# Three dense tiles' expert gates added to a DRAM table by GpSimd instead of built from one-hot products

## What is computed

```python
q = (h @ w_q).reshape(T, 8, 2, 128)
s = einsum('thpd,hpnd->thpn', q, sub_keys)            # scores of 2 x 128 sub-keys, 8 heads
vals, idx = top_k(s, 16)
cand = vals[:, :, 0, :, None] + vals[:, :, 1, None, :]
top_s, top_pos = top_k(cand.reshape(T, 8, 256), 16)
experts = i1 * 128 + i2                                # 16 of 16,384 experts per head
gates = softmax(top_s)                                 # (T, 8 * 16)
a = gelu(einsum('td,ted->te', h, u_tab[experts]))
y = einsum('te,ted->td', gates * a, v_tab[experts])
x = x + gate2 * rmsnorm(y)
```

## Time and profile before

| | us |
|---|---|
| runs | 2873.4, 2895.03, 2897.18 |
| median | 2895.03 |
| span of the profiled execution | 2847.3 |
| TensorE busy in it | 2774.5 |
| VectorE busy | 2158.4 |
| GpSimd busy | 1313.3 |
| ScalarE busy | 1249.3 |

### The profile page before, as it was taken

How to read it: one execution, slowest core, us unless ns; L and a number is a source line. 1 busy time by engine, 2 the same in 40 slices (tenths; PEclk the granted TensorE clock), 3 DMA queues, 4 the chain that set the end, 5 groups by cost and what they waited for, 6 DMA issues and landing times.

```text
span 2847.3 us, 43522 instructions
## 1 busy us (share of the span) xinstructions
PE 2774.5 (97%) x15948; PEld 2538.1 (89%) x15948; DVE 2158.4 (76%) x3708; ACT 1249.3 (44%) x2302; POOL 1313.3 (46%) x1036
## 2 busy tenths in 40 slices
PE   6998999999999999999999999999999999999998
PEld 5776778889999999999999999999998887877786
DVE  7655545887668778678989898777768878887888
ACT  4333662233357767744454544445522233332233
POOL 0002000000000000177878887777778888888884
PEclk9998999999999999999999999999999999999999
DMA  7520223225556566589898999899999999999996
GB/s 281 227 71 31 89 75 111 69 78 177 182 177 211 200 203 205 185 286 316 301 329 301 314 303 331 308 331 311 321 361 380 359 333 345 374 341 356 341 358 262
DMA packets 328417, 721.37 MB, mean 253 GB/s; under 512 B 44000, under 2 KB 159840, under 8 KB 326368
## 3 DMA queue, kind: packets, MB, share of 16 engines
q1 hardware_dynamic: 238176, 451.18, 44.9%
q0 software_dynamic: 90112, 268.76, 27.3%
HBM read 605.50 MB, written 114.30 MB: 253 GB/s over the span
## 4 chain that ended last, share of the span: by engine, by line
PE 57%; POOL 18%; issue 5%; DVE 2%; ACT 1%; DMA 1%; DVEq 0%; SPq 0%; ACTq 0%; POOLq 0%
PE mix L1434 47%; POOL picked_act L1872 9%; POOL rows L1879 9%; PE mix L116 5%; PE sps_all L1929 2%; PE sps_all L1947 1%; PE mix L1947 1%; ACT onehot L1641 1%; PE sps_all L1521 1%; DMA rows<-in_v,eidx 0%; DVE lo L106 0%; DVE onehot L1723 0%; DMA wq_raw<-in_w_q 0%; DVEq L1123 0%; ACT hi L101 0%
## 5 line engine op out<-in xcount | busy, mean ns | idle before, releaser
L1872 POOL DMA_INDIRECT picked_act<-act_early,aidx x384 | 467.0, 1216 | 1043.0 <-PE mix L1434 938.5
L1434 PE MATMUL mix<-a_hi,hi 128*128 128x320 f32 (+1 forms) x3072 | 810.1, 318 | 2.0 <-DVE lo L106 1.9
L1434 PE MATMUL mix<-a_lo,hi 128*128 128x320 f32 (+1 forms) x3072 | 808.8, 317 | 0.0
L1434 PE MATMUL mix<-a_hi,lo 128*128 128x320 f32 (+1 forms) x3072 | 808.5, 317 | 0.0
L1879 POOL DMA_INDIRECT rows<-in_v,eidx x512 | 651.3, 1272 | 166.4 <-issue 133.2
L1782 DVE SCALAR_TENSOR_TENSOR ys<-rows,coef,ys 128x1024 f32<-128x1024 f32 x504 | 633.9, 1284 | 118.6 <-DMA rows<-in_v,eidx 105.3
L106 DVE TENSOR_TENSOR lo<-raw,hi 128x1024 fp32r<-128x1024 f32 x384 | 469.2, 1222 | 301.4 <-ACT hi L101 301.0
L101 ACT ACTIVATE hi<-raw 128x1024 fp32r<-128x1024 f32 x384 | 404.8, 1054 | 358.3 <-PE mix L1947 348.3
L1434 PEld LDWEIGHTS mix<-a_hi,hi 128*128 128x128 f32 x3072 | 533.6, 188 | 3.2 <-ACT gelu L1650 2.3
L1434 PEld LDWEIGHTS mix<-a_lo,hi 128*128 128x128 f32 x3072 | 535.1, 188 | 0.0
L1434 PEld LDWEIGHTS mix<-a_hi,lo 128*128 128x128 f32 x3072 | 534.7, 188 | 0.0
(11 more groups left out here) (268 smaller groups left out, 3899.3 us busy)
## 6 DMA issues: line engine op xcount, KB each, us to landing
raw<-in_u SPq DMA_DIRECT2D x256, 512.0 KB, 4.9
raw<-in_v SPq DMA_DIRECT2D x128, 512.0 KB, 6.0
act_late<-gelu SPq DMA_DIRECT2D x128, 320.0 KB, 4.6
act_in<-act_late SPq DMA_DIRECT2D x128, 256.0 KB, 6.5
act_early<-gelu SPq DMA_DIRECT2D x128, 192.0 KB, 1.8
gate_d<-free_lo SPq DMA_DIRECT2D x19, 1024.0 KB, 8.1
gt<-gate_d SPq DMA_DIRECT2D x64, 256.0 KB
free_lo<-gate_d SPq DMA_DIRECT2D x64, 256.0 KB, 7.6
```

Of the source, the lines that this page charges most:

```text
L1434: done = pe.matmul(dst, w, a[:, k, cols], start=first, stop=last)
L1872: pool.indirect_dma_start(out=g.picked_act[:, e:e + 1], out_offset=None, in_=act_tables[e // (EARLY * CHOSEN)], in_offset=bass.IndirectOff ...
```

## The change

The gates of dense tiles are built in two ways instead of one. The dense tiles are now tiles 0 to 3 and the gathered ones 4 to 7. The tiles handled in retrieval (0 to 2) are thereby dense. For these GpSimd adds each gate, by an indirect transfer of one float for each of 128 tokens with an adding write, to a zeroed table in DRAM: 3 tiles x 8 heads x 16 choices = 384 transfers. The table lies beside the activations (`act_gates`, 512 activation columns and 384 gate columns per key and expert), so one load of 448 KB a step (`ag_in`) brings both. Tile 3 keeps the one-hot products: 16 batches, steps 49 to 94. Its gates are loaded as before, 64 KB a step. L1809's one multiplication becomes two (384 and 128 columns).

Four transfers on ScalarE's queue zero the table during the projections, and a GpSimd memset makes their source. The gates of the first tiles are finished by pairs of heads (`shift_heads`, `exp_heads`, `finish_heads`), three pairs in retrieval and the last in steps 6 to 8. Before head h of a tile is added, the previous head's sixteen transfers must have landed. Rows start at step 147 instead of 133; 2.5 fall in a step up to 255 (272 in all) and 1.9 behind it. Buffers move; the semaphores of the attention stage are freed and cleared behind it.

```diff
-HEAD_TILES = EARLY
+HEAD_TILES = DENSE - 1
+HEAD_GROUP = 2
+HEAD_EXPS_AT = (7, 11, 15)
...
+SCATTERED = HEAD_TILES
+AG = DTOK + SCATTERED * P
+ZERO_TILES, ZERO_COLS = 64, 192
+ZERO_FILLS = N // ZERO_TILES * SCATTERED * P // ZERO_COLS
+ZERO_AT = (3, 4, 5, 6)
+DENSE_FROM = 2 * N - 8
...
-ROWS_FROM, PICKS, BEATS = 133, 4, 4
-ROW_EVERY = (5 / 12, 7 / 12)
+ROWS_FROM, PICKS, BEATS = 147, 4, 4
+ROW_EVERY = (2 / 5, 10 / 19)
...
+            def clear_gates(j):
+                rows, part = divmod(j, SCATTERED * P // ZERO_COLS)
+                cols = slice(DTOK + part * ZERO_COLS, DTOK + (part + 1) * ZERO_COLS)
+                tables = g.act_gates[rows * ZERO_TILES:(rows + 1) * ZERO_TILES, :, cols].rearrange("n p c -> p n c")
+                if j == 0:
+                    act.wait_ge(g.zeros_ready, 1)
+                act.dma_start(tables, g.zeros[:].unsqueeze(1).to_broadcast([P, ZERO_TILES, ZERO_COLS])).then_inc(g.zeros_stored, 16)
...
+def finish_heads(g, dve, b):
+
+    gates = g.gates_d[:, 0:HEAD_TILES, group_heads(b), :]
+    norm = g.norm[:, 0:HEAD_TILES * HEAD_GROUP].rearrange("p (c h) -> p c h", h=HEAD_GROUP)
+    dve.wait_ge(g.heads_exps, b + 1)
+    dve.tensor_reduce(norm, gates, AX, ALU.add)
+    for h in range(HEAD_GROUP * b, HEAD_GROUP * (b + 1)):
+        dve.scalar_tensor_tensor(g.sidx[:, 0:HEAD_TILES, h, :], g.chosen_r[:, h, :, :, 1], float(NKEYS), g.chosen_r[:, h, :, :, 0],
+                                 ALU.mult, ALU.add)
+    dve.drain()
+    dve.reciprocal(norm, norm)
+    for c in range(HEAD_TILES):
+        slots = g.sidx[:, c, group_heads(b), :]
+        dve.tensor_scalar(slots, slots, float(AG), g.gate_col[:, c:c + 1], ALU.mult, ALU.add)
+    dve.drain()
+    dve.tensor_tensor(gates, gates, norm.unsqueeze(3).to_broadcast([P, HEAD_TILES, HEAD_GROUP, TOPK]), ALU.mult)\
+       .then_inc(g.scatter_ready, 1)
...
-    rows = 12 * (min(m, late) - ROWS_FROM + 1) // 5
-    return min(GATHERED * CHOSEN, rows + max(0, m - late) * 12 // 7)
+    rows = 5 * (min(m, late) - ROWS_FROM + 1) // 2
+    return min(GATHERED * CHOSEN, rows + max(0, m - late) * 19 // 10)
...
-        pieces = lambda a: a[:].rearrange("p (k j t) -> p k j t", k=KC, t=GTOK)
-        gates = g.gt[n // GROUP % 2].rearrange("p k (j n t) -> p k j n t", n=GROUP, t=GTOK)[:, :, :, n % GROUP, :]
-        dve.tensor_tensor(pieces(g.cf[n % 2]), gates, pieces(g.act_in[n % ACTS]), ALU.mult)\
-           .then_inc(g.cf_ready, 1)
+        both, cols = g.ag_in[n % ACTS], slice(SCATTERED * P, DTOK)
+        dve.tensor_tensor(g.cf[n % 2][:, 0:SCATTERED * P], both[:, 0:SCATTERED * P], both[:, DTOK:], ALU.mult)
+        pieces = lambda a: a.rearrange("p (j t) -> p j t", t=GTOK)
+        gates = g.gt[n // GROUP % 2].rearrange("p j (n t) -> p j n t", t=GTOK)[:, :, n % GROUP, :]
+        dve.tensor_tensor(pieces(g.cf[n % 2][:, cols]), gates, pieces(both[:, cols]), ALU.mult).then_inc(g.cf_ready, 1)
...
+    def scatter_gates(t, head):
+        if head:
+            pool.wait_ge(g.scattered[t], 16 * TOPK * head)
+        for k in range(TOPK):
+            pool.indirect_dma_start(out=gate_table, out_offset=bass.IndirectOffsetOnAxis(ap=g.sidx[:, t, head, k:k + 1], axis=0),
+                                    in_=g.gates_d[:, t, head, k:k + 1], in_offset=None, compute_op=ALU.add)\
+                .then_inc(g.scattered[t], 16)
+
+    for head in range(HEADS):
+        if head == 0:
+            pool.wait_ge(g.zeros_stored, 16 * ZERO_FILLS)
+        if head % HEAD_GROUP == 0:
+            pool.wait_ge(g.scatter_ready, head // HEAD_GROUP + 1)
+        for t in range(HEAD_TILES):
+            scatter_gates(t, head)
```

372 lines of the change are left out of this document (194 added, 178 removed).

## The result

Four runs of the changed kernel took 2997.3 to 3009.6 us, median **2999.6**; the kernel before took 2889.8 in the median of four. The ratio is **1.0396, 95% interval 1.036 to 1.0432**: slower by 4%. (The ratios are estimated from the single runs; the quotient of the medians can differ by a tenth or two of a per cent, and is 1.038 here.) The forecast was 2928 us and a range up to 2990.

A forecast was written before the change was run, and what follows sets the result against it. TensorE was taken to bound the kernel, with GpSimd setting the pace after the change. Terms -47 + 3 + 0 + 0 + 20 + 67 = +43, taken as +33: span 2880, plus 47.7 gives 2928 us, range 2846 to 2990.

The forecast's parts named there:

- What bounds the kernel: Whole kernel: TensorE, busy 97% of the span, so work taken off it shortens the span if its feeding engine keeps up.
- Removed from TensorE, -47: First and second sweep: 48 of 64 gate batches and three transposes go, 9.5 us in the first and 36.5 in the second.
- Retrieval, +3: Retrieval: VectorE's gate finishing per two heads takes about 3 us a group; only the third group is not hidden.
- Zero fills, 0: Projections: four 6.3 MB fills, 17 us of DMA each, cost nothing as weights load a tile ahead; upper end 68 us.
- The sign named for this: Projections: TensorE waiting on weights between 120 and 190 us would show the zero fills costing time.
- The scatters, 0: From 518 us: 384 adds at 1.49 us end near 1090, harmless up to 1.99 us each; 38 us per 0.1 beyond.
- Second sweep, +20: Second sweep: rows need a gather per 1.41 us, GpSimd takes 1.49; lateness between 0 and 35 us.
- Dense sweep, +67: Dense sweep: 468 gathers at 1.63 us plus 14 make 777 us against 710; range 0 to +123.
- Minus 10 for shared lateness: Second and dense sweeps: 10 us of the second's lateness is the same the dense would meet, so +43 becomes +33.
- 47.7 us outside the span: Whole kernel: the runs' median 2895.0 lies 47.7 us above the profiled span; the same was added to the forecast span.
- Scatters outlast the first rows: Rival, second sweep: at 2.2 us a scatter, rows start 80 us late, giving 3010 us; chance 0.10, including a costly fill.
- The rival of no change or faster: Dense sweep: GpSimd keeps up at a gather of 1.48 us, giving 2851 us, faster by 1.5%; chance 0.24.

The follow-up runs named there:

- a_no_scatters: The changed kernel without its 384 adding transfers and the waits for them (gates of three tiles missing): 2918.1 against 2853.5 us of the kernel before, 1.0229.
- two_scattered: A kernel computing the whole output: tiles 0 and 1 scattered, 2 and 3 by one-hot products, fills in pieces, against the kernel before: 2848.3 against 2855.7 us, 0.9979.
- a_third: The changed kernel, unedited, on a chip of the faster kind: 2943.7 against 2855.7 us of the kernel before, 1.0294.
- b_again: The kernel before, unedited, profiled and timed once more on a chip of the faster kind: 2855.5 us.
- a_fills_pieces: The changed kernel with its zero fills in 32 transfers of 0.79 MB from GpSimd, each after the last landed: 2929.4 against 2856.7 us of the kernel before, 1.0264.
- a_rows_151: The changed kernel with rows from step 151 instead of 147 and 2 instead of 1.9 in a dense step: 2948.2 against 2856.7 us of the kernel before, 1.0318.
- b_third: The kernel before, unedited, profiled on a chip of the slower kind: 2897.5 us.
- a_again: The changed kernel, unedited, on a chip of the slower kind: 3013.2 against 2897.7 us of the kernel before, 1.0386.
- b_rows_147: The kernel before with only the changed kernel's row schedule (rows from step 147 instead of 133): 2945.4 against 2853.5 us, 1.0328.
- a_one_input: The changed kernel with two VectorE instructions of a dense step reading one SBUF input instead of two (low products wrong): 2990.9 us against 3013.2 unedited.

## Why the prediction was wrong, step by step

On an A chip the parts can be set beside the forecast's: taken off TensorE 42 us (forecast 47), retrieval and fills +35 (3), second sweep +27 (20), dense sweep +74 (67), and nothing for shared lateness (-10). Together +94 in the span, forecast +33. Of these 61 us the fills are 32, more than half; the forecast's mechanism, that GpSimd sets the pace from the second sweep on, was right and its two large terms were each 7 us short.

*What bounds the kernel.* Right: in a_no_scatters and two_scattered what is taken off TensorE in the second sweep arrives in full, 901.1 instead of 938.3 us.

*Removed from TensorE, -47.* Right in the second sweep: -37.2 for 38 batches and three transposes. In the first sweep 5.2 arrive instead of 9.5. The rest is lost in the sweep's first 43 us, where TensorE is busy 37.1 us instead of 41.0 (a_third, b_again); why was not tried.

*Retrieval, +3.* It can't be read apart from the fills. With both it is +34.6, and +5.9 in a_fills_pieces, so +3 is not contradicted.

*Zero fills, 0.* **Failed, +34.6 or nearly.** I argued that a weight load a tile ahead absorbs being late by 17 us. The size was about right (25.17 MB at the stretch's 348 GB/s are 72 us in all, I had 68), the cover wasn't: the fills come one behind the other at 84, 97, 117 and 137 us, and TensorE waited 31.5 us for `w_lo`. The sign named for this, TensorE waiting on weights between 120 and 190 us, came. What runs showed instead: four fills delay the sweeps by 25 to 41 us at each of four places, and 28.7 us go with the same bytes in 32 pieces, one at a time. So it is not the bytes as such, and hardly the place.

*The scatters, 0.* **Failed by a term of its size.** I took 1.49 us each and named 1.99 as the limit of what does no harm. They took 1.742 + 0.304 = 2.05. The floor is 1.55 instead of the pick's 0.94. Started at 560 instead of 518 (35 of these 42 us are the later start of everything), they end at 1346, and the first row comes at 1364 instead of 1303. Of these 61 us 37 are the later start of the second sweep, the fills above all; against the steps the row is 24 us late (its due point, step 145.5, is at 1340). By my own rule of 38 us for each 0.1 us beyond the limit I would have had 23 us more; measured: 23 to 27 (a_no_scatters against a_third). The rule was about right, the price wrong. What the scatters cost on a B chip no pair of runs shows.

The line of the Trainium skill that I quoted against these adds (DMA: Bandwidth & Descriptors, Specifications: below 512 B a DMA engine reads, modifies and writes) speaks of the DMA engines, prices nothing and says nothing of GpSimd's time. By GpSimd's time the add does cost more than the plain write, 1.55 against 0.95 us. For the rest of the core it is the plain writes, at 1.3 us apart, that are the costly ones. Whether such a read and write takes place no run shows.

*Second sweep, +20.* The reason was wrong and the size near, which is luck. I had 1.19 us for a gather there; it took 1.13 in a_third and 1.10 to 1.11 in a_no_scatters and a_rows_151 (from 1400 us on), with issue 1.41, which is what the schedule wants. With rows on time none of the steps is late (a_no_scatters, a_rows_151: 0 us). The 27 us on an A chip go with the late first row.

*Dense sweep, +67.* **Right**: 74.3 on an A chip; on B chips 63.3 (the result's own profile against b_third) and 83.6 (a_again against it). The count was 465 instead of 468, a gather 1.645 to 1.70 instead of 1.63, and what follows the last gather 24 us instead of 14. b_rows_147 shows the whole of it by the schedule alone (+76.7). The reason given for 1.65, gathers held by VectorE's instructions with two SBUF inputs, was too narrow: a_one_input shows that one with one input holds them too.

*Minus 10 for shared lateness.* Not seen. The sweeps' losses add up.

*47.7 us outside the span.* **Failed.** Each run has 1.8 us there. I joined a span of one chip to a median of another. The forecast's increment doesn't hang on it, but the 40 us of a B chip are no constant either: the issue idle in them grows from 20 us to between 51 and 58.

*Chances.* "Scatters outlast the first rows" had 0.10 and only at 2.2 us; fills shared it. Both came, and together with the forecast's own mechanism. The range ended at 2990, below the 3010 us that this rival gave by itself, and had no room for two of these on top of each other. The rival of no change or faster needed a dense gather of 1.48; it was 1.65.

## What to carry to other kernels

Before work is moved to an engine, count that engine's budget to the end: here each gather put off costs 1.65 us and each scatter 2.05. A tile's 128 scatters take 262 us of GpSimd to save 16 of TensorE (16 batches of 0.96 us), and that pays only in time in which nobody else wants GpSimd. Price a bulk transfer by the small transfers that come behind it, not by its share of the bandwidth: cut in pieces, each issued when the one before had landed, the same bytes cost 6 us and not 35. And take the time outside the span from the run that was profiled, never from another.

## What the hardware showed that I had not expected

- Small writing transfers of GpSimd, one in about 1.3 us, nearly stop the core while the DMA engines are at 0.10: TensorE does one product in 0.6 us (655 to 862 us) to 2.8 us (950 to 1118), with nothing to wait for in the profile. The granted clock is at its lower level, 1.2 GHz (0.50) from 950 to 1000 us, where TensorE was busy 7 us of 50; it had been 1.00 before the scatters. With drains and memsets between them, at one in 4.0 us, and with adding ones at one in 2.05, nothing of the kind. What is starved no run shows. A like pattern appears for short times on B chips while GpSimd's gathers run packed, 1.25 us apart: 58 us of idle in a_again, 20 in b_third, none on an A chip at the same density. Why chips differ is open.
- An adding scatter of one float for each of 128 tokens holds GpSimd 1.55 us undisturbed, a plain one 0.95, as long as a gather.
- The 8 KB transfer that took 27.6 us behind a fill of 6.3 MB had been issued from another queue than the fill. So a transfer of one engine can wait behind that of another. The Trainium skill (DMA: Bandwidth & Descriptors, "Issuing engines are not separate DMA queues") says that transfers of all engines run on the same 16 DMA engines and interleave. The trace agrees with the sharing; interleaving did not save this one. At 0.79 MB the next piece can go out 4.73 us behind the one before.
- For the wait of a gather for VectorE the Trainium skill's remark (SBUF — State Buffer, "Who interferes with whom") that tensor_tensor does not stall descriptor generation is inferred there. Here the `lo` subtraction, a tensor_tensor with both inputs in SBUF, held the 114 gathers of a_third that started inside it until it had ended (each ends 0.80 to 0.83 us behind it), so the measurement decides against the remark in this kernel. The one-input tensor_scalar of a_one_input held them in the same way.
